# A first phase recorded and laid out by a list scheduler, with four-partition LayerNorm sums, a compact Toeplitz load and a staged prefetch

## The reference

```
def mixer_ab(x, ...):
    xr, yr, cv, cg = split(x @ w_in)                 # 1024 -> 4 x 512
    xc = causal_dwconv(xr, width 4)                  # "rec conv"
    h  = rg_lru(xc)                                  # gates, then a linear recurrence over time
    rec_out = h * gelu(yr)
    g  = cv * sigmoid(cg)
    c  = causal_dwconv(g, width 31)                  # "conformer conv"
    c  = silu(layer_norm(c, cf_g, cf_beta))          # over the 512 channels
    return concat([rec_out, c]) @ w_out
def rg_lru(x):                                       # per channel
    r, i = sigmoid(x @ ga + ba), sigmoid(x @ gx + bx)
    a = exp(-8 r softplus(-lam));  u = sqrt(1 - a*a) * (i * x)
    h[t] = a[t] * h[t-1] + u[t]
```

## Time and profile before

| | us |
|---|---|
| median of 3 runs | 6545.52 |
| lowest, highest | 6545.35, 7014.72 |
| the profiled execution's own time | 6546.69 |
| its span on the slowest core (core 0) | 6544.9 |
| spans of the 8 cores | 6528.9 to 6544.9 |
| PE, DVE, ACT, POOL busy in it | 5933.3, 3396.1, 2712.7, 1946.2 |

### The profile page before, as it was taken

One profiled execution on the slowest core, in us unless ns is written; L12 is line 12 of the kernel. 1 busy time (PEld: TensorE's weight loads), 2 busy tenths in 40 slices (PEclk: granted clock), 3 DMA queues, 4 the chain that ended last, 5 costly groups with the idle time before them and its releaser, 6 DMA issues.

```text
span 6544.9 us, 128981 instructions; the slowest of 8 cores (6528.9 to 6544.9 us)
## 1 busy us (share of the span) xinstructions
PE 5933.3 (91%) x36386; PEld 2873.7 (44%) x36386; DVE 3396.1 (52%) x6822; ACT 2712.7 (41%) x5509; POOL 1946.2 (30%) x1444
## 2 busy tenths in 40 slices
PE   3878778599999999999999999999999999999998
PEld 1434434244454444444444444444444444444444
DVE  2565665546463636363636363636363636363562
ACT  2545455324343435343434343434343434343442
POOL 1333332332323132314141414141323232323213
PEclk7888888699999999999999999999999999999999
DMA  7645641344444444545454444444444444445434
GB/s 118 86 66 82 81 67 39 122 158 148 149 133 156 155 152 146 172 146 171 148 169 159 162 160 158 158 158 158 158 158 158 158 161 155 161 158 164 153 118 135
DMA packets 236897, 919.02 MB, mean 140 GB/s; under 512 B 30076, under 2 KB 30980, under 8 KB 223910
## 3 DMA queue, kind: packets, MB, share of 16 engines
q1 hardware_dynamic: 204406, 740.33, 34.6%
q0 software_dynamic: 31792, 170.44, 13.1%
HBM read 931.01 MB, written 93.33 MB: 157 GB/s over the span
## 4 chain that ended last, share of the span: by engine, by line
PE 71%; DVE 9%; ACT 9%; issue 6%; DMA 2%; POOL 2%; DVEq 0%; ACTq 0%; SPq 0%; POOLq 0%
PE ps L426 68%; PE ps L434 3%; ACT L451 2%; DVE p_xc L465 2%; ACT pbf L451 2%; DVE sbb L465 1%; ACT pT L451 1%; DVE p_ii L649 1%; POOL ccb L454 1%; DVE smA L973 1%; ACT p_a L451 1%; DMA gtmp<-st_cf 1%; DVE p_xc L461 1%; DVE ccb L454 1%; DVE ccb L586 1%
## 5 line engine op out<-in xcount | busy, mean ns | idle before, releaser
L426 PE MATMUL ps<-xT,ring 128*128 128x512 bf16 x12544 | 2813.0, 380 | 4.7 <-ACT s_sg L451 1.1
L426 PEld LDWEIGHTS ps<-xT,ring 128*128 128x128 bf16 x12544 | 1189.1, 98 | 1397.1 <-issue 28.5
L454 POOL TENSOR_TENSOR res<-res,lnt 128x1024 f32<-128x1024 f32 x512 | 1204.3, 2352 | 659.3 <-ACT res L451 568.4
L426 PE MATMUL ps<-ring,hT 128*128 128x512 bf16 x5632 | 1286.0, 383 | 14.7 <-ACT vbuf L451 14.7
L461 POOL TENSOR_SCALAR res<-res,sm 128x1024 f32<-128x1024 f32 x192 | 230.3, 1199 | 2316.8 <-ACT xnb L451 2304.3
L451 ACT ACTIVATE sgt<-ps 128x512 f32<-128x512 f32 x704 | 417.0, 592 | 1110.9 <-PE ps L426 1108.7
L426 PEld LDWEIGHTS ps<-ring,hT 128*128 128x128 bf16 x5632 | 535.8, 98 | 640.3 <-issue 38.7
L426 PE MATMUL ps<-axT,win 128*128 128x512 bf16 x2048 | 563.2, 438 | 196.8 <-DVE ccb L586 125.1
L451 ACT ACT_TABLE_LOAD x278 | 356.7, 1283 | 828.8 <-DVE sm L751 458.2
L454 DVE TENSOR_TENSOR hT<-sgt,ps 128x512 bf16<-128x512 f32 x330 | 227.0, 688 | 825.2 <-PE ps L426 813.0
L465 DVE SCALAR_TENSOR_TENSOR res<-res,ps 128x512 f32<-128x512 f32 x512 | 328.4, 683 | 456.0 <-PE ps L426 455.9
(11 more groups left out here) (201 smaller groups left out, 5061.8 us busy)
## 6 DMA issues: line engine op xcount, KB each, us to landing
ring<-tape SPq DMA_DIRECT2D x1280, 512.0 KB, 4.2
lnt<-lntab POOLq DMA_DIRECT2D x62, 1024.0 KB, 8.0
tape<-tape POOLq DMA_DIRECT2D x80, 512.0 KB, 24.4
res<-x SPq DMA_DIRECT2D x64, 512.0 KB, 7.4
y<-res POOLq DMA_DIRECT2D x64, 512.0 KB, 7.1
axnb<-x POOLq DMA_DIRECT2D x64, 256.0 KB, 6.2
qT<-roc_d SPq DMA_DIRECT2D x16, 1024.0 KB, 8.8
toep<-toep POOLq DMA_DIRECT2D x4, 2048.0 KB, 22.1
```

Of the source, the lines that this page charges most:

```text
L426: P.op("pe", lambda e: e.matmul(out, lhsT, rhs, start=start, stop=stop), [lhsT, rhs], [out], start=start)
L454: P.op(eng, lambda e: e.tensor_tensor(out, a, b, op), [a, b], [out])
```

## The change

The first phase is no longer emitted in the order of the loop body. `P.begin()` makes every operation a record with an assumed duration; `P.schedule()` then plays all five engines forward and gives each engine, whenever it is free, the oldest record whose inputs are ready. Activations that use the same function table are kept in groups that may not overtake each other. The result is a fixed order again.

What else changes in the first phase:

- The convolution gets PSUM banks 4 and 5 for itself; all other rotating results share banks 0 to 3.
- Sums: 32 fp32 matmuls of 128 columns with a 4-column selector, so that the sum for the 512 frames lies on 4 partitions x 128; mean and variance are worked out there, and 8 fp32 matmuls of 128 columns spread them over 128 partitions again.
- From DVE to POOL: the first operation of the width-4 convolution and the product in `rec`. From DVE to ACT: the copy of the three carried frames. From POOL to ACT and DVE: two small state copies. ACT also copies the spread mean.
- The Toeplitz matrices are loaded without their zeros (four casts of 0.5 MB) and spread by 16 masked copies, 8 on ACT, 8 on DVE.
- The stores to `roc_d` are issued by POOL and ACT, not SP. The ring is loaded in stages during the last iteration (`pump(2)`, `pump(4)`, `pump(8)`, `pump()`), and `load_res(0)`, `load_roc(0)` move ahead of the last item's normalization. The ring's slots are counted from another start, so that the first pieces go where `axnb` lies.

```diff
+    def schedule(self, hop=0.2):
...
+            for e in self.ENGS:
+                if not ready[e]:
+                    continue
+                t = max(free[e], min(a for a, _ in ready[e]))
+                if nxt is None or t < nxt[0]:
+                    nxt = (t, e)
+            t, e = nxt
+            at, idx = min((x for x in ready[e] if x[0] <= t), key=lambda x: x[1])
...
+        for t, n, r in out:
+            if r.is_dma:
+                r.real = self.dma(r.eng, r.semkey[4:], r.fn, r.reads, r.writes)
+            else:
+                r.real = self.op(r.eng, r.fn, r.reads, r.writes, r.start)
...
-            ts_op("dve", xc[:, 0:n], xr_[:, 0:n], w(0), pcol[:, C_RCB + c:C_RCB + c + 1], ALU.mult, ALU.add)
+            ts_op("pool", xc[:, 0:n], xr_[:, 0:n], w(0), pcol[:, C_RCB + c:C_RCB + c + 1], ALU.mult, ALU.add)
...
-            stt(a2[:, 0:n], ii[:, 0:n], 0.5, a2[:, 0:n], ALU.mult, ALU.mult)
+            tt_op("pool", a2[:, 0:n], ii[:, 0:n], a2[:, 0:n], ALU.mult)
...
-            b = banks.next()
+            b = ps[4 + c % 2]
...
-        def stats(c):
-            mm(s1[:, 0:n], ones[:, :], cc[:, c, 0:n], c == 0, c == 3)
-            mm(s2[:, 0:n], ones[:, :], sqb[:, c, 0:n], c == 0, c == 3)
+        def stats(src, bank):
+            for c in range(4):
+                for q in range(nqb):
+                    mm(bank[0:4, 0:nq], onee[:, 3 - q:7 - q], src[:, c, q * nq:(q + 1) * nq],
+                       c == 0 and q == 0, c == 3 and q == nqb - 1)
...
+        def spread(bank, row):
+            for q in range(nqb):
+                mm(bank[:, q * nq:(q + 1) * nq], sels[q], row, True, True)
...
+    def toep_fill(c):
+        v = toep[:, c, :].rearrange("p (a q t) -> p a q t", q=4, t=32)
+        src = toepc[c].rearrange("p (a t) -> p a t", t=32)
+        for q in range(4):
+            msk = pcol[:, C_MASK + q:C_MASK + q + 1]
+            if q % 2:
+                act(v[:, :, q, :], src, AF.Identity, bias=onee[:, 0:1], scale=msk)
+            else:
+                ts_op("dve", v[:, :, q, :], src, msk, None, ALU.mult)
...
-    abank = Banks([0, 1, 2, 3, 4, 5])
+    abank = Banks([0, 1, 2, 3])
...
         else:
+            load_res(0)
+            load_roc(0)
+        if i == M - 1:
             pump()
```

More of the change, by code:

```diff
@@ L43 @@
     __slots__ = ("eng", "fn", "waits", "semkey", "seq", "needs_inc", "value", "is_dma")
+class Rec:
+    __slots__ = ("eng", "fn", "reads", "writes", "start", "semkey", "is_dma", "cost", "done", "group", "idx", "preds", "succs", "left", "real")
 class Prog:
@@ L146, in _add_waits, with free, note @@
             op.waits.append(rop)
-    def op(self, eng, fn, reads=(), writes=(), start=True):
+    def free(self, ap):
+        n = 1
+        for s_, k in list(ap.ap)[1:]:
+            n *= int(k)
+        return n
+    def note(self, eng, fn, reads, writes, start, cost, done, semkey, is_dma):
+        r = Rec()
+        r.eng, r.fn, r.reads, r.writes, r.start, r.semkey, r.is_dma = eng, fn, list(reads), list(writes), start, semkey, is_dma
+        r.cost, r.done, r.group, r.idx, r.real, r.preds, r.succs, r.left = cost, done, self.group, len(self.buf), None, set(), [], 0
+        if self.anchor is not None:
+            r.preds.add(self.anchor)
+        self.buf.append(r)
+        return r
@@ L149, in op @@
+    def op(self, eng, fn, reads=(), writes=(), start=True, cost=None):
         if self.dry:
             return None
+        if self.buf is not None:
+            if cost is None:
+                n = max(self.free(writes[0]), self.free(reads[0]) if reads else 0)
+                cost = {"pe": 0.02 + n / 2400.0, "act": 0.18 + n * 0.00105, "dve": 0.08 + n * 0.0012,
+                        "pool": 0.1 + n * 0.0023, "sp": 0.1}[eng]
+            return self.note(eng, fn, reads, writes, start, cost, cost, eng, False)
@@ L450, in act @@
             wr.append(accum)
-        P.op("act", lambda e: e.activation(out, in_, func, **kw), rd, wr)
+        tab = TABLES.get(func)
+        cost = 0.18 + P.free(in_) * 0.00105
+        if tab is not None and tab != act_tab[0]:
+            cost += 1.28
+            act_tab[0] = tab
+            act_tab[1] += 1
+        P.group = None if tab is None else ("act", act_tab[1])
+        P.op("act", lambda e: e.activation(out, in_, func, **kw), rd, wr, cost=cost)
+        P.group = None
     def tt_op(eng, out, a, b, op):
@@ L512, in take @@
             pump()
-        return [ring[(p0 + i) % RING] for i in range(len(pids))]
+        return [ring[slot(p0 + i)] for i in range(len(pids))]
     def drop(pid):
@@ L585, in dtr @@
     def dtr(out, in_):
-        P.op("dve", lambda e: e.transpose(out, in_), [in_], [out])
+        P.op("dve", lambda e: e.transpose(out, in_), [in_], [out], cost=0.72)
     def head(ab, t, is_last, oi, banks):
@@ L687, in norm @@
                 tt_op("pool", cc_, cc_, mean, ALU.subtract)
-                tt_op("dve", cc_, cc_, var, ALU.mult)
+        def norm():
+            for c in range(4):
+                cc_ = cc[:, c, 0:n]
+                tt_op("dve", cc_, cc_, s2[:, 0:n], ALU.mult)
         def silu():
@@ L716, in head @@
         J.ab, J.t = ab, t
-        J.xr, J.glu, J.gates, J.yr, J.root, J.rec, J.conv, J.stats = xr, glu, gates, yr, root, rec, conv, stats
-        J.moments, J.varroot, J.norm, J.silu, J.store_ro, J.outs = moments, varroot, norm, silu, store_ro, outs
+        J.xr, J.glu, J.gates, J.yr, J.root, J.rec, J.conv, J.sums = xr, glu, gates, yr, root, rec, conv, sums
+        J.conv_turn, J.conv_bias, J.spread_mean, J.spread_rstd = conv_turn, conv_bias, spread_mean, spread_rstd
+        J.moments, J.varroot, J.center, J.norm, J.silu, J.store_ro, J.outs = moments, varroot, center, norm, silu, store_ro, outs
         J.is_last = is_last
@@ L1099, in _build @@
                 x_tr(nx.ab, nb, abank)
+            if i == M - 2:
+                pump(2)
+        if i == 0:
+            toep_fill(0)
+            toep_fill(1)
         if p1:
-            for c in range(4):
-                p1.stats(c)
+            p1.sums()
             p1.moments()
@@ L1315, in _shared_inputs @@
     pcol = np.zeros((128, NCOL), f)
+    for q in range(4):
+        pcol[32 * q:32 * q + 32, C_MASK + q] = 1.0
     rcw = inp["rec_conv_w"][0]
```

260 lines of the change are left out of this document (187 added, 73 removed).

## The result

In two of the four executions of each kernel the cores of one die or of both ran at a lower clock, for which my sum has no term: they lift the median over all four of the change to 6356.9 us, above my range, and say nothing about the change, so I compare the other two, 6227.25 and 6227.68 us against 6545.35 and 6545.52 before, a ratio of 0.951 with the 95% interval [0.947, 0.956]. Against 6227 the forecast of 6170 is 57 us too low. What follows is about those 57 us, and about where the 318 us came from.

What follows compares the result with a forecast made beforehand. An order making engines wait for each other was taken to bound the first phase. Start, periods and end, 175.5 + 961.7 + 138.9, become 100 + 723 + 77, 376 us less: 6170 us forecast, range 6105 to 6300.

Steps and rivals of the forecast that it cites:

- the slower case: First phase's sums and spreads: narrow fp32 matmuls have a high floor, making the kernel slower, about 6700 us; chance 3%.
- three rivals that give the gain back: First phase: late results hold PE (19%, 6295 us), clock held down (8%, near 6290), order does nothing (4%, 6375).
- no period is 60 us: First-phase periods: fixed order meets other durations, a late result holds PE, period 60 to 62, 6295 us; chance 19%.
- a list that does nothing: First-phase periods: Toeplitz and prefetch parts work, the order does nothing, period near 67, 6375 us; chance 4%.
- a dense PE: First phase: the clock is held down at 0.81 when PE is dense, time near 6290 us; chance 8%.
- The period: 14 first-phase periods between tile 1's and tile 15's projections: 13 of 52 us, first 47, 723 for 961.7, -239 us.
- the 2 us that I added to PE's work: Period's second half: allowance for DVE as close second where glu of block 2 needs a bank, 50 to 52 us.
- four state copies, about 1: DVE's work per tile: state copies newly put on DVE, about 1 us, within its forecast 34 us.
- The start: Up to tile 1's first projections: near 100 us instead of 175.5, -75 us (55 to 90).
- subtracting one wait: Sample's item at the start: 51 us before, 29 without the Toeplitz wait, plus 9 for the masked copies.
- The end: From tile 15's projections to `projA(0)`: 77 us in place of 138.9, -62 us (40 to 72).
- the last chain: At the end: moments, root, reciprocal and spread without cover, 5 to 10 us.

Runs made afterwards that it cites:

- Full sums: The change with LN statistics on 128 partitions as before, sums of 512 columns and no spreading matmuls: 0.951 [0.950, 0.953] of the kernel before.
- written order: The change without its list scheduler, every operation issued in the order in which the loop body is written: slower than the kernel before, by 99 us.
- the shortest kernel: The change with statistics on 128 partitions, the carried columns' copy on ACT and all masked Toeplitz copies on DVE: 6188 us, 0.945 of the kernel before.

## Why the prediction was right and wrong

**What held.** All of the effect lies in the first phase; the second is as it was. PE's work of a tile was forecast as 50.2 us at full clock and is 49.7 in the period at clock 1.00. A record of the narrow sums takes 0.11 us (3.66 for 32), so the slower case falls. ACT has 37.4 us (38 forecast), DVE 35.7 (34), POOL 32.1 (29.6). PE is the engine that binds, and core 1's periods are 52.6 us on average at a clock of 0.96 where I said 52 and over 0.95. Of the three rivals that give the gain back none came: no period is 60 us; a list that does nothing would have been 6375 us, and without it the time is over the kernel before; and with a dense PE on all eight cores a whole period ran at 1.00. On that last point this trace goes against the Trainium skill's rule (TensorE: Matmul & The Clock Gate, Seeing it yourself) of 13/16 for a die with three dense cores. Before the change the case is less clear, which I had not seen. I read the 0.78 of the earlier trace rows on core 0 alone; the other cores but core 1 had 0.85 there, because cores 0 and 1 stood at 0.81 for 253 us of the first phase while the others did not. Core 0, then core 2:

```profile
565.00:596.00 31.00, 29.12 (x181) 14.33 (x180) 16.42 (x26) 17.37 (x25) 10.81 (x18) 0.81 0.90 115
```

```profile
565.00:596.00 31.00, 24.64 (x175) 12.78 (x175) 16.62 (x27) 17.57 (x24) 10.29 (x18) 0.99 0.92 112
```

That is the rule's clock, but on two cores of the die and not on all four. In the profiled execution of the change no core is at 0.81 at any time.

**The period (52 forecast, 54.1 on the slowest core, +34 us): the step that failed.** The term that was mis-sized is the 2 us that I added to PE's work for all waits and half clock: on the slowest core they are 68 us in 14 periods, 4.9 each. It has two places. "On: ... four state copies, about 1" took the copies on DVE for short work and asked nothing about who runs beside them. They took 2.0 us per tile (25.5 over 13 tiles), and stood in front of work that PE waits for; with the copy on ACT and the list that came with it the whole kernel is 24 us shorter, most clearly at the end. I had weighed the interplay of POOL and DVE for the products alone. There it was real too: the 168 products of `p_xc` went from 751 ns, their mean in the kernel before, to 1043, which gives back 3.5 us per tile of the 5.7 that the moved operations took off DVE, while the products of `norm`, with one input in PSUM, went from 1112 to 667. In the kernel with those operations back on DVE the products of `p_xc` take 784. This agrees with the Trainium skill (GPSIMD Engine Reference, 1. Specifications), which I cited, and applied only to the products of `norm` and `p_a`.

The other place is "I add 2 us for it ... and the half clock should be nearly gone". On core 6 the 14 periods are some 690 us of work (13 of 49.7 and the first, some 44, an estimate), 40 of waits and, as what is left, 28 of half clock; I had 26 for both, 2 per period. 18.3 of the 40 are stalls without a releaser, which the kernel before hardly had. That its own waits hid them is my reading: I had no row to price them from, and did not ask what supplies PE's instructions at a higher rate.

**The start (100 forecast, 119.4).** Item 0 ended at 71 instead of 62: PE waits 5.7 us for `p_xcb` and 3.1 for the scaled piece, steps that I had run without gaps. Taking the scaling out ended item 0 earlier, but did not start tile 1 earlier on core 0. The sample's item took 48 us instead of 38, at a clock of 0.67. I had called ACT an engine with little to do there, and it was busy 37.5 of 48.4 us; yet freeing it gave 3 us. So the miss was to scale a chain of short steps from the 51 us of before by subtracting one wait; which of its steps is worth the rest stays open.

**The end (77 forecast, 85.9).** My sum gave PE 2 us of stalls, 5 to 10 for the last chain, and nothing to half clock. On core 6 its waits are 13 us in all, 3.9 of them behind DVE's copy, at a granted clock of 0.86. The narrow sums are not what the forecast missed: with them kept the end is 74.7 us when the copy is on ACT, and 76.3 (core 1) when the list is planned with measured costs, both under 77. Full sums, with the lists that come with them, still take 16 us off this stretch with the copy on DVE and 9 with it on ACT. How much of the 9 us is the copy's and how much the order's stays open.

**What the parts were worth.** I gave each part its own microseconds. The experiments say that the list carries the change: without it the other parts lose 99 us in written order, with it own banks bring 35, the compact load 10 to 22 and the narrow sums nothing, each with the list that came along. The staged prefetch was never taken back, so what it is worth is not shown.

## What to carry to other kernels

When an operation is moved to an engine that "has time", look at what the neighbours run in that moment: a copy of 32 columns waited for POOL's instructions to end, in front of a bank that PE wanted, and moving it made three kernels 24 to 34 us shorter. A generated order with the prefetch is worth over half of this gain, but small edits of it cost 8 to 32 us, so a part is only weighed with the list held still; of my parts only the casts were. And when the bound engine stops pausing, price what its pauses hid, here the supply of its instructions.

## What the runs showed of the hardware that was not expected

- A bf16 copy of 128 x 32 on DVE takes at most 177 ns while POOL is idle and up to 6.4 us while POOL runs without a break. With full sums on core 1, each copy of over 0.5 us ends within 0.05 us of the end of a POOL instruction, and five of the six of over 4 us end with POOL's whole run: such a copy is blocked, not slowed. Not every copy is: six that began and ended inside a POOL instruction took 0.17 to 0.18 us.
- PE stalls without a releaser are 0 to 2.4 us per core before, 0 to 2.0 in the written order, 5 to 24 in the change, 31 to 50 in the shortest kernel (all between 23 and 950 us), and 5.6 to 10.5 in the change when half of the casts' traffic is gone under the same list. They do not go by density alone: 24 to 34 with measured costs, whose periods are 56 us.
- The sample's item ran at a granted clock of 0.67 though PE had work in 33 of its 48 us, while a period with PE busy 95% of the time was granted 1.00.
- In one execution of the kernel before, two cores of a die stood at a granted clock of 0.81 for 253 us while the other two were at 0.88 and 0.99 (565 to 596 us), and from tile 1 to `projA(0)` these two took 1100 us, the other six cores 1091 to 1096.
